# Thirteen kinds of eight unused products behind the first output tile of the last feed-forward block

## The reference, cut to what matters

```python
D_MODEL = 1024; SEQ = 256; D_FF = 2816

f = rms_norm(h, ffn_norm_g[l]) @ w_up[l]            # 1024 -> 2 x 2816
f = depthwise_conv(f, ffn_dw_w[l], ffn_dw_b[l])     # 3 taps over the tokens
fg, fu = jnp.split(f, 2, axis=-1)
h = h + (jax.nn.silu(fg) * fu) @ w_down[l]          # 2816 -> 1024
```

## Time and profile before

| what | value |
|---|---|
| the two runs shown | 1333.8 and 1337.12 us, median 1335.46 us |
| span of the profiled execution | 1332.1 us, from the first to the last instruction |
| around the span in these runs | 1.7 to 5.0 us (run minus span) |
| TensorE busy | 1305.4 us (98%), 8104 products |
| GpSimd, ScalarE, VectorE busy | 707.6, 685.5, 573.3 us |
| DMA | 210.16 MB |

### The profile page before, as it was taken

How to read it: one execution, slowest core, us unless ns; L and a number is a source line. 1 busy time by engine, 2 the same in 40 slices (tenths; PEclk the granted TensorE clock), 3 DMA queues, 4 the chain that set the end, 5 groups by cost and what they waited for, 6 DMA issues and landing times.

```text
span 1332.1 us, 22086 instructions
## 1 busy us (share of the span) xinstructions
PE 1305.4 (98%) x8104; PEld 1089.2 (82%) x8104; DVE 573.3 (43%) x1093; ACT 685.5 (51%) x1096; POOL 707.6 (53%) x307
## 2 busy tenths in 40 slices
PE   5999999999999999999999999999999999999999
PEld 1688567787888888888777757999999987999999
DVE  3423683225544344301146365455532485456620
ACT  4561345334544444422247745666665667766652
POOL 1432004352544444445336212688899775888897
PEclk8999999999999999999999999999999999999999
DMA  9532634471322332443544252665566541565564
GB/s 364 185 95 95 260 134 161 147 279 48 126 94 94 96 101 99 155 166 110 162 153 138 79 206 80 216 192 199 192 202 211 174 143 48 196 197 192 191 206 125
DMA packets 60132, 210.16 MB, mean 158 GB/s; under 512 B 6432, under 2 KB 9760, under 8 KB 59936
## 3 DMA queue, kind: packets, MB, share of 16 engines
q1 hardware_dynamic: 59632, 207.52, 45.9%
q10 hardware_dynamic: 432, 1.70, 0.3%
HBM read 208.15 MB, written 1.05 MB: 157 GB/s over the span
## 4 chain that ended last, share of the span: by engine, by line
PE 93%; DVE 3%; ACT 1%; DMA 1%; SPq 1%; issue 1%; ACTq 0%; DVEq 0%
PE ps L352 74%; PE ps L479 2%; PE ps L407 1%; PE ps L1117 1%; PE ps L389 1%; PE ps L399 1%; PE ps L1501 1%; DMA raw<-wstream 1%; PE ps L1132 1%; PE ps L1480 1%; PE ps L1124 1%; SPq L314 1%; PE ps L1111 1%; PE ps L1483 1%; PE ps L498 1%
## 5 line engine op out<-in xcount | busy, mean ns | idle before, releaser
L341 POOL TENSOR_TENSOR wlo<-raw,whi 128x1024 fp32r<-128x1024 f32 x291 | 695.3, 2406 | 609.2 <-ACT whi L336 608.7
L336 ACT ACTIVATE whi<-raw 128x1024 fp32r<-128x1024 f32 x291 | 306.5, 1056 | 213.2 <-PE ps L352 148.1
L352 PE MATMUL ps<-Hhi_,whi 128*128 128x256 f32 (+1 forms) x1336 | 388.5, 319 | 0.0
L352 PE MATMUL ps<-Hlo_,whi 128*128 128x256 f32 (+1 forms) x1336 | 385.0, 316 | 0.0
L352 PEld LDWEIGHTS ps<-Hhi_,whi 128*128 128x128 f32 x1336 | 251.0, 188 | 22.2 <-issue 4.1
L352 PEld LDWEIGHTS ps<-Hlo_,whi 128*128 128x128 f32 x1336 | 251.0, 188 | 19.4 <-issue 1.4
L352 PE MATMUL ps<-Hhi_,wlo 128*128 128x256 f32 (+1 forms) x1336 | 231.8, 316 | 0.0
L352 PEld LDWEIGHTS ps<-Hhi_,wlo 128*128 128x128 f32 x1336 | 194.5, 188 | 18.1
L352 PE MATMUL ps<-hidhi,whi 128*128 128x256 f32 (+1 forms) x528 | 151.1, 315 | 0.0
L352 PE MATMUL ps<-hidlo,whi 128*128 128x256 f32 (+1 forms) x528 | 150.7, 314 | 0.0
L775 ACT ACTIVATE u<-ps,par 128x256 f32<-128x256 f32 (+1 forms) x132 | 83.9, 635 | 114.7 <-PE ps L352 101.3
(11 more groups left out here) (334 smaller groups left out, 1575.2 us busy)
## 6 DMA issues: line engine op xcount, KB each, us to landing
raw<-wstream SPq DMA_DIRECT2D x367, 512.0 KB, 3.5
Haside_lo<-wstream SPq DMA_DIRECT2D x8, 512.0 KB, 5.7
Haside_hi<-wstream SPq DMA_DIRECT2D x8, 512.0 KB, 9.2
Paside<-wstream SPq DMA_DIRECT2D x4, 512.0 KB, 4.9
XT<-x_t SPq DMA_DIRECT2D x1, 1024.0 KB, 10.0
XT<-ctx_t SPq DMA_DIRECT2D x1, 1024.0 KB, 12.2
memx<-mem_t ACTq DMA_DIRECT2D x1, 1024.0 KB, 5.8
out_t<-XT SPq DMA_DIRECT2D x1, 640.0 KB, 6.1
```

What stands on the lines that cost most here:

```text
L336: nc.scalar.activation(whi[:, n % RING, :], raw[:, r % RAWS, :], ACT.Copy).then_inc(S["hi_ready"], 1)
L341: nc.gpsimd.tensor_tensor(wlo[:, r, :], raw[:, r, :], whi[:, n % RING, :].bitcast(F32), ALU.subtract).then_inc(S["lo_ready"], 1)
L352: mm = nc.tensor.matmul(o, a, b, start=start, stop=stop)
```

## The change

A new function `row_reads` is called in `ffn_pe` behind the three parts of tile 0 of the last feed-forward block (`f == 2 and m == 0`). It issues 13 kinds of 8 products with F32R operands. The stationary operand is a block of `hidlo1` (four blocks in turn, so each product loads weights), the moving operand a view of `hidhi1`, and every product is a sum of its own (`start=True, stop=True`) in bank 7, whose result nobody reads. The kinds, in order: (1) 512 elements in a row; (2) the same with the two halves taken in turn; (3) every second of 1024; (4) one element 512 times; (5) pieces of 16 from the two halves, in the order a, l, e; (6) four pieces of 128, 256 apart; (7) 480, (8) 256 and (9) 128 in a row; (10) every fourth of 2048; (11) every sixteenth, wrapping; (12) as 1 with 64 output columns; (13) as 1 with 64 rows.

```diff
+        def row_reads(pe):
+
+            flat = hidhi1[:, :, :].rearrange("p k t -> p (k t)")
+            row = flat[:, 0:512]
+            rows = [row,
+                    row.rearrange("p (a t) -> p t a", a=2),
+                    flat[:, 0:1024].rearrange("p (t a) -> p t a", a=2)[:, :, 0],
+                    flat[:, 0:1].to_broadcast([P, 512]),
+                    row.rearrange("p (l a e) -> p a l e", a=2, e=16),
+                    hidhi1[:, 0:4, 0:P],
+                    flat[:, 0:480],
+                    flat[:, 0:256],
+                    flat[:, 0:128],
+                    flat[:, 0:2048].rearrange("p (t a) -> p t a", a=4)[:, :, 0],
+                    row.rearrange("p (l e) -> p e l", e=16)]
+            for x in rows:
+                o = ps[:, 7, 0:x.free_size()]
+                for i in range(8):
+                    nc.tensor.matmul(o, hidlo1[:, i % 4, 0:P], x, start=True, stop=True)
+            for i in range(8):
+                nc.tensor.matmul(ps[0:64, 7, :], hidlo1[:, i % 4, 0:64], row, start=True, stop=True)
+            for i in range(8):
+                nc.tensor.matmul(ps[:, 7, :], hidlo1[0:64, i % 4, 0:P], flat[0:64, 0:512], start=True, stop=True)
+
         def ffn_pe(pe, f, ntok, norm):
...
                         pe.wait_ge(S[f"{t}_free"], 48)
                         mod_products(pe, 1, DN0_UNITS[3 * m + part_])
+                if f == 2 and m == 0:
+                    row_reads(pe)
                 if f == 1 and m == 1:
```

## The result

The changed kernel takes 1363.36 us (1363.26 and 1363.45), the kernel before 1335.46 us (1333.8 and 1337.12): ratio 1.0214, 95% interval [1.0195, 1.0233]. That is slower by 27.9 us where 26.4 was forecast, inside the range, on the border of two per cent. Between the two profiled executions the span grew by 29.5 us, from 1332.1 to 1361.6 us; of the two runs of before, one was 3.3 us above the other. On another occasion the same two kernels stood at 1365.23 us (4 runs) and 1333.84 us (7 runs), ratio 1.023 [1.0213, 1.0247].

The account below looks back on a forecast made before the run. TensorE's order was taken to bound the kernel's end: 21.6 us for the added products at pattern-free prices plus 4.8 us for far reads, 26.4 us, giving 1361.9 us around the median of 1335.5 us. The range was 1355 to 1375 us.

Parts of the forecast that it names:

- TensorE's order bounds the end of the kernel, and all of the block lands on it: Last down projection: TensorE is always busy, so the added products' whole 26.4 us come out at the end.
- Rivals 4 and 5: Last down projection: added work fills TensorE's waits (1335 us), or unused products are dropped (1335.5 us); chance 0.03 together.
- A full row costs 226.7 ns, by columns: Added block: 512 columns take 226.7 ns and 256 exactly half, 113.3 ns; ten 512-column kinds sum to 18.14 us.
- 128 columns take 0.111 us, set by the loads: Added block's 128-column kind: weight loads set 0.111 us a product, 0.89 us in all, ends 0.5 to 1.8 us.
- The half-size kinds don't pair: Added block's 64-output-column and 64-row kinds: the full 0.2267 us a product; pairing would take off 1.6 us.
- The far patterns cost about double: Added block: halves in turn, every fourth and every sixteenth take 0.427 us a product, adding 4.8 us; chance 0.42.
- every second element I leave at full pace: Added block's every-second kind: no extra cost for elements 8 bytes apart; upper end 0.427 us each, 1.6 us.
- the step that put "the two halves taken in turn" among the far ones: Added block: successive elements 1 KB apart were taken to cost 0.427 us a product instead of 0.2267.
- Rival 1: Added block: the read pattern does not matter, one element per cycle; 21.6 us, 1357.1 us in all; chance 0.25.
- rival 3: Added block: one lost cycle per new 64-byte piece, every fourth differing from every sixteenth; 25.1 us, 1360.6 us; chance 0.13.
- Rival 2: Added block: supply limited by 16-byte pieces, one element per piece costing four times; 38.2 us, 1373.7 us; chance 0.17.
- 7.48 us per tile after: Tiles behind the added block: they keep the earlier pace of 7.48 us each, with no idle before them.

Follow-up runs that it names:

- the plain-row block: The changed kernel with its block replaced by 104 products of 512 elements in a row and no other kind; 1365.85 us in a single run.
- the block of sums of 16: The changed kernel with its block replaced by 8 kinds of 16 products, each kind one sum, in a row or in turn; 1354.77 us in a single run.
- the fastest kernel: The kernel before, without the block, reading rows in turn in the first feed-forward block and the other two down projections; 1314.45 us, ratio 0.9854.

## Why the prediction was right, and where it was not

- *TensorE's order bounds the end of the kernel, and all of the block lands on it.* Right: no hole in the chain, the helpers' waits alone grew. Rivals 4 and 5 are out. The tiles behind the block did not get shorter, and the 104 products are all in the trace.
- *A full row costs 226.7 ns, by columns.* Right for 512 in a row (226.6 in the settled part of the plain-row block, 1.84 us for 8 with the first ones at 228 to 236). For 256 it was 119 ns here, and 120 in the block of sums of 16: neither the 113.3 of the earlier trace rows nor the 117.8 behind the block. So the price "exactly half" holds for one pace of several.
- *128 columns take 0.111 us, set by the loads.* 0.106 measured. The columns alone (0.057) are excluded as the price of the row of 8, but the first interval is 61 ns. That fits the loads, if the first one was done beside the longer product ahead; no run shows the loads as the cause.
- *The half-size kinds don't pair.* Right, and their extra 0.4 us is for the most part at the changes of size.
- *The far patterns cost about double.* The size was right for two of the three kinds, 434 and 461 ns against 427. The sorting failed: the step "every second element I leave at full pace" was wrong by 1.8 us, and the step that put "the two halves taken in turn" among the far ones by 1.7 us the other way. The two misses cancel, so the block's sum owes its closeness (27.4 against 26.4 us) partly to luck. With only one of the two kinds put right, at the forecast's own prices, its sum would have been 24.8 or 28.0 us. What I sorted by, the distance of two successive elements, is not what matters; the groups of four and the number of rows in turn are.
- The Trainium skill's note on cachelines ("SBUF — State Buffer", "Door 1: The DMA port swizzle") asks for two hits per 16-byte line. Every second element has two hits a line, and so have two of every four; both cost 450 ns here. Two rows in turn change the line at each access, and cost 216. The measurement differs from the rule in both, and it decides.
- The Trainium skill's N / 2.4 + 2.5 ns ("TensorE: Matmul & The Clock Gate", "Back-to-back issue gap"), which that section gives for an isolated product, is met to 0.1 ns by 512 columns as two rows in turn (215.8) and is not by the same row read straight (226.7). By it the forecast's sum would be 1.0 us smaller, not 0.9.
- Rival 1 (pattern free) and rival 3 (a cycle per new piece of 64 bytes) fall with every second element at 450 ns; rival 3 also wanted every fourth at 267. Every fourth does differ from every sixteenth, which was to be rival 3's sign, but the other way round (461 against 434 ns). Rival 2 (four times for every fourth) falls with 461.
- *"7.48 us per tile after"* was wrong: 7.77, 2.05 us in all. This step was never a term of the sum; I had taken for granted that the same instructions keep their pace. It is the larger part of what the two traces differ by beyond the forecast (29.5 - 26.4 = 3.1 us, of which 1.0 is the block and 0.1 the first interval behind it).
- *"1.7 to 5.0 us lie around the span."* Not so: in each of the runs whose span is listed, 1.7 to 1.9 us lie around it. If the longer run of before was like them, its extra 3.3 us lay inside its span.
- The median of before was made of two runs 3.3 us apart. Against the shorter of them, or the 1333.84 us of the later ones, the change is 29.6 to 31.4 us; a stretch at 117.8 ns a product, in a part that the change doesn't touch, is of this size.

## What to carry to other kernels

A stream of rounded 32-bit products is paced by how its moving row is read: keep groups of four elements together, and if the row holds two halves, read them in turn and let the readers of PSUM undo the order; here that was worth 10.9 ns of 226.7 for each product, 1.3% of the kernel. Don't step by two inside the row: it cost double here (450 against 227 ns). And before two versions that differ by a few microseconds are compared, look at the spacing of equal products in both traces: it may be another step of the same stream.

## What had not been expected of the hardware

TensorE's stream of loads and products with 256 columns runs in one of at least two steps, 113.3 or 117.8 ns a product, at the same granted clock (1.00), and stays in it for 100 us and more. (The block's own products with 256 columns in a row have a third, 119 to 120 ns.) In the same code of one and the same kernel, both were seen. Eight plain rows of 512 brought the slow one in each of the three traces in which they stood directly ahead of a tile, and so did eight products with 64 rows in their three; a plain float32 product behind the block brought the fast one both times. Four other kinds (every fourth, 128, 480, 64 output columns) brought or kept the fast one. A plain product doesn't bring it always: in the fastest kernel a row of plain products ends at 1015.4 us and the next 90 products take 117.8 ns each. What the two steps are, I can't tell from these runs; that reading two rows in turn avoids both (111.6 ns) points to the reads. That those of the rows and of the weights get in each other's way would be a guess, since no run takes the loads away. The number of rows in turn that TensorE reads without loss lies at two, and is below four; three was not tried.
